# One fp32 diffusion trunk: modulation products moved to VectorE, the head on half the contraction, the router's norm by blocks

## The reference, cut to what matters

```
h = x * (1 + scale) + shift
x = LayerNorm(alpha * x + gate * sublayer(h))
```

## Time and profile before

| | |
|---|---|
| median of 3 runs | 1898.12 us (1897.44 to 1901.23) |
| profiled execution, its own time | 1892.98 us |
| its span | 1890.8 us |
| mean granted TensorE clock | 0.97 |
| busy: PE, DVE, ACT, POOL | 1755.0, 782.6, 665.5, 28.7 us |
| moved from and to HBM | 480 MB, mean 254 GB/s |

### The profile page before, as it was taken

How to read it: one execution, slowest core, us unless ns; L and a number is a source line. 1 busy time by engine, 2 the same in 40 slices (tenths; PEclk the granted TensorE clock), 3 DMA queues, 4 the chain that set the end, 5 groups by cost and what they waited for, 6 DMA issues and landing times.

```text
span 1890.8 us, 24131 instructions
## 1 busy us (share of the span) xinstructions
PE 1755.0 (93%) x9428; PEld 1216.8 (64%) x9428; DVE 782.6 (41%) x1220; ACT 665.5 (35%) x961; POOL 28.7 (2%) x52
## 2 busy tenths in 40 slices
PE   6999999899999998999768999999899999999997
PEld 3885557688888776976556556655555566565553
DVE  2334553623323255644653443333441433433344
ACT  3224554423222234324634333333334333333241
POOL 2200000000000000000000000000000000000000
PEclk9998999899999999999888999999999999999999
DMA  9734752232322544321009999999989999999986
GB/s 342 162 110 169 259 174 71 67 108 90 117 95 90 202 176 167 112 89 45 5 27 385 421 416 421 421 421 385 421 354 386 385 415 421 420 421 399 413 351 258
DMA packets 111471, 481.81 MB, mean 255 GB/s; under 512 B 8154, under 2 KB 46216, under 8 KB 62208
## 3 DMA queue, kind: packets, MB, share of 16 engines
q1 hardware_dynamic: 108192, 470.57, 63.8%
q0 software_dynamic: 3168, 9.71, 2.1%
HBM read 477.38 MB, written 2.87 MB: 254 GB/s over the span
## 4 chain that ended last, share of the span: by engine, by line
PE 71%; DVE 11%; DMA 8%; ACT 6%; issue 3%; SPq 0%; DVEq 0%; ACTq 0%
PE PS L762 18%; PE PS L764 17%; PE PS L763 17%; DMA RAWB<-in_w_exp_up 5%; PE PS L1254 4%; PE PS L1327 3%; PE PS L784 2%; ACT BH L1753 2%; DVE RAWAL L2407 2%; PE PS L944 1%; PE PS L1202 1%; ACT S L1509 1%; PE PS L954 1%; DMA RAW<-in_w_mod 1%; ACT S L1548 1%
## 5 line engine op out<-in xcount | busy, mean ns | idle before, releaser
L1881 DVE TENSOR_TENSOR WL<-RAW,WH 128x2048 fp32r<-128x2048 f32 (+1 forms) x63 | 142.1, 2256 | 316.1 <-ACT WH L1455 316.0
L762 PE MATMUL PS<-HH,WH 128*128 128x512 f32 (+1 forms) x584 | 225.0, 385 | 5.7 <-DVE HL L1940 4.6
L763 PE MATMUL PS<-HL,WH 128*128 128x512 f32 (+1 forms) x584 | 222.2, 380 | 0.0
L764 PE MATMUL PS<-HH,WL 128*128 128x512 f32 (+1 forms) x584 | 222.1, 380 | 0.0
L1455 ACT ACTIVATE WH<-RAW 128x2048 fp32r<-128x2048 f32 (+1 forms) x63 | 118.8, 1887 | 259.6 <-PE PS L764 228.6
L762 PE MATMUL PS<-BH,HE 128*128 128x512 f32 x448 | 182.2, 407 | 22.4 <-DVE RAWAL L2407 17.0
L2407 DVE TENSOR_TENSOR RAWBL<-RAWB,BH 128x2048 fp32r<-128x2048 f32 x42 | 96.3, 2292 | 211.0 <-ACT BH L1753 211.0
L764 PE MATMUL PS<-BH,LE 128*128 128x512 f32 x448 | 176.5, 394 | 0.0
L1753 ACT ACTIVATE BH<-RAWB 128x2048 fp32r<-128x2048 f32 x42 | 80.4, 1914 | 231.8 <-DMA RAWB<-in_w_exp_up 138.5
L2407 DVE TENSOR_TENSOR RAWAL<-RAWA,BH 128x2048 fp32r<-128x2048 f32 x42 | 96.1, 2289 | 144.8 <-ACT BH L1753 144.8
L762 PEld LDWEIGHTS PS<-BH,HE 128*128 128x128 f32 x448 | 84.7, 189 | 87.2 <-issue 33.9
(11 more groups left out here) (313 smaller groups left out, 2723.9 us busy)
## 6 DMA issues: line engine op xcount, KB each, us to landing
RAWA<-in_w_exp_up SPq DMA_DIRECT2D x112, 1024.0 KB, 10.2
RAWB<-in_w_exp_up SPq DMA_DIRECT2D x112, 1024.0 KB, 9.8
RAWA<-in_w_exp_down SPq DMA_DIRECT2D x56, 1024.0 KB, 9.8
RAWB<-in_w_exp_down SPq DMA_DIRECT2D x56, 1024.0 KB, 9.2
RAW<-in_w_mod SPq DMA_DIRECT2D x48, 1024.0 KB, 5.0
RAW<-in_w_ffn_up SPq DMA_DIRECT2D x22, 1024.0 KB, 5.1
RAW<-in_w_in_c SPq DMA_DIRECT2D x12, 1024.0 KB, 5.1
RAW<-in_w_ffn_down SPq DMA_DIRECT2D x10, 1024.0 KB, 6.8
```

Source lines behind the costliest of these rows:

```text
L762: mm(ps, ah, bh, start=start, stop=False)
L763: mm(ps, ah, bl, start=False, stop=False)
L764: return mm(ps, al, bh, start=False, stop=stop)
L1881: v.tensor_tensor(WL[:, c % 2, 0:n], raw("weight", c)[:, 0:n], WH[:, c % 2, 0:n].bitcast(F32), ALU.subtract).then_inc(s_lo, 1)
```

## The change

Of 24 blocks, four stay in the head on PE, in the order 0, 2, 1, 3. The other 20 are multiplied and added by DVE straight from the raw chunk: for each of 4 slices of 128 rows of the contraction and each stream one operation of 512 columns adds slice times silu(c) (a scalar per partition) to a sum MSUM of 128 x 512, the first one a plain multiply. What is then left, a sum over partitions, is done by PE with the sum as stationary operand and a column of ones: four matmuls per stream (`sum_columns`), and DVE adds the bias. Six blocks are placed in projection of layer 0, eleven in feed-forward up (one in each stage, blocks from 16 on with one stream), three in feed-forward down. PE waits for these at the marked places.

The head multiplies the first half of the contraction for the first four tiles (chunks 0 and 1, which have a buffer RAWF of their own, loaded early) while blocks 1 and 3 of the modulation are landing. Tokens are turned before the modulation, copied by ACT and modulated in SBUF by ACT and DVE in halves, and they are loaded from SP's queue in place of POOL's.

The last residual norm before the router works by blocks of 128 tokens; its learned scale and shift go into the router's modulation (`fold_router`), and POOL applies them to X beside the router. ACT and DVE share the copies of the router's and of the experts' gathered inputs, the first big expert chunk is split ahead, and SP reads one expert number at a time. The gate matmuls of feed-forward down move from unit 0 to unit 3.

```diff
-MOD_PRE, MOD_ATT, MOD_DOWN = 4, 13, (5, 2)
+MOD_PRE, MOD_IN, MOD_UP, MOD_DN = 4, 6, FT // 2, 3
...
+        def mod_streams(n):
+
+            return (0, 1) if n < 16 else (0,)
...
+        for part in (("mod", 0), ("mod", 1), ("mod", 2), ("weight", 0), ("mod", 3), ("weight", 1),
+                     ("mod", 4), ("mod", 5), ("mod", 6), ("mod", 7)):
...
+        mod_in = {2: (8, 9), 3: (10, 11), 4: (12, 13), 5: (14,), 6: (15, 16), 7: (17,), 8: (18, 19)}
+        mod_down = {0: (42,), 1: (43,), 4: (44,), 5: (45,), 8: (46,), 9: (47,)}
...
+            sp.wait_ge(s_tab, 1)
 
             def load_experts(i, phase):
                 e = {}
-                for n, who in enumerate((0, 1, 2, "big")):
-                    e[who] = sp.value_load(TAB[0:1, bass.ds(i + (TE + n * NI), 1)], min_val=0, max_val=NE - 1)
                 for q, (who, what, st, h) in enumerate(order):
                     if (what == "d") != (phase == "down"):
                         continue
+                    if who not in e:
+                        n = 3 if who == "big" else who
+                        e[who] = sp.value_load(TAB[0:1, bass.ds(i + (TE + n * NI), 1)], min_val=0, max_val=NE - 1)
...
+            for b in (2, 3):
+                xb = X[:, b, :]
...
+                gp.tensor_tensor(xb, xb, LNR[:, 0, :], ALU.mult).then_inc(s_gpx, 1)
+                gp.wait_ge(s_gpx, b - 1)
+                gp.tensor_tensor(xb, xb, LNR[:, 1, :], ALU.add).then_inc(s_ln, 1)
...
+            def sum_columns(n, bank):
+
+                pe.wait_ge(s_macc, mod_added(2 * n + 1))
+                if bank != 1:
+                    pe.wait_ge(s_modc, col_batches[0])
+                one = CN[:, C_IOTA + 1:C_IOTA + 2]
+                for j in range(4):
+                    at = (mod_block(n) * 4 + j) * 2
+                    for s in mod_streams(n):
+                        last = mm(PS[:, bank, at + s:at + s + 1], mod_sum(n)[:, s, j * P:(j + 1) * P], one,
+                                  start=True, stop=True)
+                last.then_inc(s_modcol, 1)
+                col_batches[0] += 1
...
             pe.wait_ge(s_silu, 2)
             pe.wait_ge(s_stz, 1)
-            mod_rows(0, MOD_PRE, 2)
+            turn_tokens(range(0, 4))
+            mod_half(0, 0, 6)
+            mod_half(0, 1, 6)
+            turn_tokens(range(4, 6))
+            mod_half(1, 0, 7)
+            turn_tokens(range(6, KT))
+            mod_half(1, 1, 7)
+            mod_columns(0, 2)
+            mod_columns(1, 2).then_inc(s_modcol, 1)
+            pe.wait_ge(s_lo, 1)
+            first_half(0, 0, 0, range(0, 2))
+            pe.wait_ge(s_modrow, 1)
+            mod_half(2, 0, 6)
+            first_half(0, 0, 0, range(2, 4))
+            mod_half(2, 1, 6)
+            first_half(1, 0, 1, range(0, 4))
...
                 for kind in plan:
+                    if l == 0 and 4 <= c - c0 < 7:
+                        pe.wait_ge(s_rope, N_ROPE0)
+                        sum_columns(MOD_PRE + c - c0 - 4, 6)
                     w = split_ready(c)
...
+                        if l == 0:
+                            for n in ((7,), (8, 9))[kh]:
+                                sum_columns(n, 6)
...
-                    if i < MOD_ATT:
-                        mod_half(MOD_PRE + i, 0, 7)
...
                     if st >= 2:
                         pe.wait_ge(s_mul, 2 * (st - 1))
+                        sum_columns(MOD_PRE + MOD_IN + st - 2, st % 2 * 4 + 3)
...
+                    if i == 11:
+                        sum_columns(23, 6)
...
+                for k in range(4):
+                    for s in mod_streams(n):
+                        acc, by = mod_sum(n)[:, s, :], ST[:, 4 * kh + k, s:s + 1]
+                        if (kh, k) == (0, 0):
+                            ins = v.tensor_scalar(acc, w[:, k, :], by, None, ALU.mult)
+                        else:
+                            dve.wait_ge(s_macc, adds[0] + 1 - len(mod_streams(n)))
+                            ins = v.scalar_tensor_tensor(acc, w[:, k, :], by, acc, ALU.mult, ALU.add)
+                        ins.then_inc(s_macc, 1)
+                        adds[0] += 1
...
                     if l == 0 and i == 5:
                         mask_biases()
+                    if l == 0 and i in (4, 5, 6):
+                        sum_columns(i, 6)
+                    if l == 0 and i == 8:
+                        sum_columns(7, 6)
+                    if l == 0:
+                        for m in mod_in.get(i, ()):
+                            mod_products(m)
...
+                for m in range(20 + 2 * st, 22 + 2 * st):
+                    mod_products(m)
             product_lo(1)
...
+                if i == 11:
+                    sum_columns(23, 6)
+                for m in mod_down.get(i, ()):
+                    mod_products(m)
             norm_halves(1)
```

More of the change, by code:

```diff
@@ L367, in trunk @@
         s_landed = [sem(f"raw_landed{i}") for i in range(RING)]
+        s_early = [sem(f"first_weights_landed{i}") for i in range(2)]
         s_mland = [sem(f"expert_raw_landed{i}") for i in range(MRING)]
@@ L484, in trunk @@
         NG0 = len(groups[0])
-        assert MOD_ATT <= NG0 - 3 and MOD_PRE + MOD_ATT + sum(MOD_DOWN) == DEPTH * NB_MOD
+        assert MOD_PRE + MOD_IN + MOD_UP + MOD_DN == DEPTH * NB_MOD
         g_base = [0, NG0]
@@ L817, in h_phase, with h_router @@
                     last.then_inc(s_hps, 1)
+            def h_router():
+                for b in (2, 3):
+                    pe.wait_ge(s_xh, ln_before[2] + b - 1)
+                    for dt in range(KT):
+                        last = nc.tensor.transpose(PS[:, dt // 4 * 2 + b - 2, dt % 4 * P:(dt % 4 + 1) * P],
+                                                   X[:, b, dt * P:(dt + 1) * P], ident)
+                        if dt % 4 == 3:
+                            last.then_inc(s_hps, 1)
             def h_halves(h):
@@ L871, in fill @@
                     def fill(ps):
-                        for k in range(KT):
+                        for k in range(4 if l == 0 and t[0] < 4 else 0, KT):
                             if t[0] == t0:
@@ L1466, in mod_row_out, with tokens_out, modulate_first @@
                     .then_inc(s_modrow, 1)
-            for n in range(MOD_PRE):
-                mod_row_out(n, n % 2)
-            act.wait_ge(s_lam, 1)
-            fn(LT[:, 2:4], LT[:, 0:2], ACT.Exp).then_inc(s_lame, 1)
+            def tokens_out(dts):
+                for dt in dts:
+                    act.wait_ge(s_hps, dt + 1)
+                    fn(F[:, dt, :], PS[:, (4, 5, 0, 1)[dt % 4], :], ACT.Copy).then_inc(s_xt, 1)
+            def modulate_first(half):
+                act.wait_ge(s_xt, KT)
+                act.wait_ge(s_modc, half + 1)
+                for dt in (4 * half + 2, 4 * half + 3):
+                    for s, lo in ((1, 0), (0, CTX)):
+                        last = fn(F[:, dt, lo:lo + 256], F[:, dt, lo:lo + 256], ACT.Identity,
+                                  bias=MODC[:, 0, dt, s:s + 1], scale=MODC[:, 0, 8 + dt, s:s + 1])
+                    last.then_inc(s_hf, 2)
+            tokens_out(range(0, 4))
+            mod_row_out(0, 6)
+            tokens_out(range(4, KT))
+            split(1)
+            mod_row_out(1, 7)
+            modulate_first(0)
+            split(2)
+            mod_row_out(2, 6)
+            mod_row_out(3, 7)
+            modulate_first(1)
             def h_phase(h):
                 l, seg = h // 2, 3 * (h % 2)
-                act.wait_ge(s_modc, 1 if h == 0 else 3 + MOD_ATT)
                 for dt in range(KT):
@@ L1484, in h_phase, with h_router @@
                     last.then_inc(s_hf, 1)
+            def h_router():
+                act.wait_ge(s_modf, 1)
+                act.wait_ge(s_hps, h_before[3] + 3)
+                for dt in range(4):
+                    fn(F[:, dt, CTX:TOK].rearrange("p (b q) -> p b q", b=2), PS[:, 0:2, dt * P:(dt + 1) * P],
+                       ACT.Identity, bias=MODF[:, 0, dt:dt + 1], scale=MODF[:, 1, dt:dt + 1]).then_inc(s_hf, 1)
             def project(l):
@@ L1659, in mixer @@
                 if l == 1:
-                    norm(2)
-            split(2)
+                    norm_router()
             mixer(0)
@@ L1698, in _ @@
                     product_hi(i + 2)
+                if i == 3:
+                    gates(1)
             root_table()
@@ L1889, in _ @@
+            split(1)
+            first_columns(0, 2)
+            dve.wait_ge(s_modc, 1)
+            dve.wait_ge(s_xt, KT)
+            first_split(0)
+            split(2)
+            first_columns(1, 3)
+            dve.wait_ge(s_modc, 2)
+            first_split(1)
             dve.wait_ge(s_small, 48)
@@ L2187, in mixer, with fold_router @@
+            def fold_router():
+                g, b = (VT[:, 112 + 8 * (4 + r):120 + 8 * (4 + r)] for r in range(2))
+                shift, scale = (MODC[:, 1, 8 * (3 + r):8 * (4 + r), 0] for r in range(2))
```

(5 more changed lines are left out.)

388 lines of the change are left out of this document (226 added, 162 removed).

## The result

The changed kernel's median is 1922.83 us (1921.16 to 1925.19, 4 runs) against 1897.78 of the kernel before (1895.39 to 1901.23, 4 runs): ratio 1.0129, 95% interval 1.0104 to 1.0155. It is 25 us slower, where I had forecast 11 slower. The profiled execution has a span of 1921.0 (before 1890.8) and a time of 1923.13; that of before lay 5 us under its median and this one does not, so the spans differ by 30.2.

What follows compares the result with a forecast made beforehand. PE bounds feed-forward, a PE, DVE and ACT chain attention, DMA the head and experts. Terms −6.6+21.8−11+15.2+1.3−6.7−2.7 = +11.3 take the median from 1898.12 to 1909.4 us, range 1892 to 1922.

Steps and rivals of the forecast that it cites:

- 3: Attention of layer 0: thirteen blocks leave PE, −14.9 us less two slow-clock spells, so −11; bounds −15 and +7.
- rival (a): Slow clock through attention as PE idles: ten more groups at 2.2 each, attention +7, total +29 or 1927; chance 10%.
- Step 1: Head: the first half of the contraction starts while other data lands, first matmul about 31.5, −6.6 us; bounds −4 to −10.
- Step 2: Projection of layer 0: six blocks' sums 11.8 on PE plus two stalls, 6.7 and 4.2, +21.8 us; bounds +12 and +26.
- The second wait of 4.2: Projection: chunk 6 on PE waits 4.2 us because DVE reads block 5's columns only behind bias masks and products.
- Step 4: Feed-forward up, PE-bound: sums for nine blocks 14.7 us plus 0.5 of stalls, +15.2; bound +18.
- rival (d): DVE becomes the bound of feed-forward up, each product 50 to 100 ns longer: +5, 1915; chance 12%.
- Step 5: Feed-forward down: seven blocks leave PE, −19.15; seam +7.8, columns +3.9, late norm +8.7; +1.3 us, bounds −8 and +4.
- Steps 6 and 7: Router −6.7 us from folded norm and shared copies; experts' start −2.7 from sooner loads and weights split ahead.
- Rival (e): GpSimd's operations hold up DVE's small steps in the router, losing up to 4 us of −6.7: 1913; chance 4%.
- (b): Faster: DVE is not late for PE, so 17.3 us of waits in projection, feed-forward up and seam vanish: 1892; chance 22%.
- (c): Nothing in sum: projection's two stalls (10.9) are hidden and the rest is as forecast, +0.4: 1898.5; chance 18%.

Runs made afterwards that it cites:

- e5_filler_gap: Changed kernel plus eight dummy matmuls a group in attention of layer 0, all behind the first two score matmuls: 1908.31 us, ratio 1.004 to the kernel before.
- e3_down: Changed kernel, feed-forward down: unit 1's low half ahead of block 20's products, block 23 summed ahead of the last unit: 1907.68 us, ratio 1.0052.
- e10_no_pool: Changed kernel with eight dummy matmuls per attention group, both feed-forward-down reorderings, and GpSimd's router operations cut to one column: 1893.4 us, ratio 0.9972.
- e2_order: Changed kernel, projection of layer 0: block 4's products behind chunk 4's split, blocks 4 to 6 summed between their chunk's two tiles: 1916.33 us, ratio 1.0096.
- e8_best: Changed kernel with 13 blocks on PE in attention, seven on DVE in feed-forward up, eight dummy matmuls in both groups without blocks: 1871.38 us, ratio 0.9835.

## Why the prediction was wrong

The direction and most terms held; the size didn't. The step that failed is 3, attention of layer 0: "Such a spell costs 2.2 a group, and −14.9 supposes none. I count two, 4 us: −11." The price of a spell was right (the slowest latent groups take 12.1 us, those of e5_filler_gap 9.6 to 9.9) and their number was not: from −14.9 to the measured +3.0 is 17.9, the price of eight and not of two. They are of unequal length; the latent groups between take 9.9 to 11.4. It was rival (a), to which I gave 10%, at +3.0 where it said +7. Its own sum was off, too: ten more groups at 2.2 are 22; its 18 is the price of eight. I had in the earlier trace rows a group with PE idle 1.69 and a clock of 0.66, and behind it one at full clock; I took the second as an even witness. The changed kernel's trace starts the stage with 20 us at 0.50 to 0.52 and then has both kinds of group in turn to its end, and e5_filler_gap shows that the idle time does it: filled with work for nobody, the stage is 134.0 us, near the 130.5 of my working without spells. The clock of its first 20 us is still 0.55 and 0.94, and I look for the other 3.5 us there; no run shows them apart.

**Step 1, head.** −3.1 and not −6.6, 0.9 outside my bounds. The first matmul came at 33.9 and not 31.5. The two blocks' columns took 3.6 us at a clock of 0.50 where I had 1.9; the kernel before shows 1.87 for one block in its head, so the row for two was there to be read. The last half block that they need was multiplied at 26.15, after a wait of 3.41 for its DMA, where I had the bytes down by 24.3: from 5 to 10 us DMA moved 264 GB/s where before it was 416. The overlap was right; the price of the columns was taken at full clock and the loads' rate too high. Nor does my 62.7 follow from its own terms: 16 steps of 0.68 from 50.1 on end at 61.0, and the text names nothing for the other 1.7.

**Step 2, projection.** +20.7 against +21.8, partly by luck. The sums (11.2) and the first wait (5.65 for 6.7) are as worked out. The second wait of 4.2 didn't come, since PE itself was 3.5 later: DVE read block 5's columns at 131.86, and PE's next sum began at 132.17. For after the 5.65 PE ran at the lower level of 1.2 GHz (granted clock 0.50 from 102.7 to 110.2), 3.4 us for the first sum in place of 1.84 and 13.2 for chunk 4 in place of 11.2. A wait of PE has to be priced with what follows it.

**Step 4, feed-forward up.** +14.4 against +15.2: no waits, 1.84 and 0.94 for the sums. Products took the row's 0.67, not more, so rival (d) falls. By the 594 ns that the prediction took from the Trainium skill ("VectorE: DVE Perf Modes", section "The TRN2 errata") they would have been faster. The same section says that this row comes out too low for single operations, and has 691 ns measured for a fp32 tensor_tensor of 512; the 0.669 measured here in a row lies between the two, and the measurement decides.

**Step 5, feed-forward down.** +2.3 against +1.3; the seam started unit 1 at 13.4 behind up's end (13.1), and two units behind it ran slow for 2 us more. e3_down takes back 14.1 of the stage by the two places named.

**Steps 6 and 7, router and experts.** −4.8 for −6.7, with slow clock in the turns and logits. Rival (e) holds as a mechanism, at 0.9 us in this trace and up to 2.9 in others (9.3 and 11.3 to the first load against e10_no_pool's 8.5), and not in the step where I had put it: it is paid between the sums and the table. From the sums to the end −5.3 for −2.7: 1.2 to the first load, 2.2 to the first big matmul, and 1.9 in the experts, where the end moves by 3 us either way between runs, so I don't explain these.

**Layer 1**, which I had at nothing, is 3.1 longer. Its code is unchanged up to the last norm, and over the traces here it takes 209.5 to 214.7 us (e2_order, e5_filler_gap and e8_best 209 to 210, less than before). Its granted clock was 0.94 in the changed kernel, 0.95 before and 0.97 in e5_filler_gap, so which of its groups ran slow seems to differ from run to run; that is argued, and no experiment was made on it. Rivals (b) and (c) fall with the waits measured.

What stays open: why two groups of e8_best ran slow behind waits of 0.70, as short as those behind which the kernel before keeps its full clock (the idle time is the cause that e5_filler_gap shows for the changed kernel, and not a rule for when a group turns slow), and how much of the head's loss is the order of the loads.

## What to carry to other kernels

Price work by the stage it leaves: where PE is not the bound and waits in small pieces, taking matmuls away can gain nothing, as here, where the clock fell with the idle time; put there what has to be done anyway (here 13 blocks, for nothing against a PE left idle), and only after that look at what an idle engine could do. A new operation on an in-order queue is priced by what stands behind it at the joints between stages: two such places cost some 14 us (feed-forward down 157.9 with them, 143.8 without), and a line moved at each gave them back. When a part of a change seems free in the average busy time, add up its load over the stretch in which it has to be done (two blocks' products in two chunks), not over the stage.

## What the runs showed of the hardware

- In traces of one execution each: eight dummy matmuls a group shortened a stage of 148.5 us to 134.0 with the granted clock from 0.77 to 0.97; twelve gave 137.3; the same eight half at another place 157.0 at 0.87.
- PE ran at a granted clock of 1.00 from 85 to 97; after 5.65 us idle it was 0.50 from 102.7 to 110.2, sums over partitions took 3.44 us in place of 1.84 and the next chunk 13.2 in place of 11.2.
- An operation of GpSimd of 128x1024 took 2.34 us, and DVE's instructions of 16 columns beside it up to 2.19 in place of 0.17 (e5_filler_gap, e10_no_pool).
